# The prologue's first three tiles over tokens 0 to 255 and 256 to 575, and its loads, transposes and splits in a new order

## What is computed

```python
def rmsnorm(x, g):
    xf = x.astype(jnp.float32)
    xf = xf * lax.rsqrt(jnp.mean(xf * xf, axis=-1, keepdims=True) + EPS)
    return (xf * g.astype(jnp.float32)).astype(x.dtype)
...
    h = rmsnorm(x, norm_mix_g)
    p = h @ w_in
    u = jax.nn.gelu(p[..., :o1])
    v = rmsnorm(jax.nn.gelu(p[..., o1:o2]), sgu_norm_g)
```

## Time and profile before

| | |
|---|---|
| median of 3 runs | 2241.7 us (2239.98 to 2243.11) |
| the profiled execution | 2245.36 us, span 2243.7 us |
| TensorE busy | 2212.0 us of the span, 99% |
| VectorE, ScalarE, GpSimd busy | 79%, 50%, 24% |
| first matmul of tile 0 | 23.34 us |
| first matmul of tile 3 | 74.80 us |

### The profile page before, as it was taken

The page is one execution under the profiler, slowest core; times in us unless marked ns, Lnnn a source line. Parts: engine busy times, 40 slices in busy tenths (PEclk is TensorE's granted clock), DMA queues, the critical chain, the costliest instruction groups (busy, mean ns, idle before and its releaser), DMA issues.

```text
span 2243.7 us, 43356 instructions
## 1 busy us (share of the span) xinstructions
PE 2212.0 (99%) x16612; PEld 2198.8 (98%) x16612; DVE 1762.5 (79%) x2354; ACT 1112.1 (50%) x1758; POOL 547.0 (24%) x685
## 2 busy tenths in 40 slices
PE   8999999999999999999999999999999999999997
PEld 8999999999999999999999999999999999999997
DVE  5777678778335998888888888888887898888886
ACT  7554444444112554445444444444444665555565
POOL 3101112212222111111111111011112355555573
PEclk9999999999999999999999999999999999999998
DMA  8334445558333244435453535353536567765433
GB/s 258 105 110 132 117 128 156 176 171 261 114 96 107 81 148 136 153 124 154 132 158 114 164 123 159 115 167 120 157 121 243 193 207 242 235 215 201 167 105 105
DMA packets 377575, 346.05 MB, mean 154 GB/s; under 512 B 10474, under 2 KB 350629, under 8 KB 372720
## 3 DMA queue, kind: packets, MB, share of 16 engines
q1 hardware_dynamic: 346608, 203.98, 31.2%
q0 software_dynamic: 30848, 140.46, 17.4%
HBM read 273.40 MB, written 71.00 MB: 153 GB/s over the span
## 4 chain that ended last, share of the span: by engine, by line
PE 61%; DMA 1%; POOL 1%; DVE 1%; issue 0%; ACT 0%; POOLq 0%
PE ps L3043 14%; PE ps L3045 13%; PE ps L3044 13%; PE ps L3104 7%; PE ps L3106 7%; PE ps L3105 7%; DMA form<-act_scratch 1%; PE ps L3118 0%; DVE w_lo L2363 0%; POOL down L1029 0%; PE ps L3162 0%; PE ps L3164 0%; PE ps L3163 0%; POOL down_s L1028 0%; POOL X L1035 0%
## 5 line engine op out<-in xcount | busy, mean ns | idle before, releaser
L3104 PE MATMUL ps<-form,dw_hi 128*128 128x288 f32 x1204 | 358.5, 298 | 5.7 <-DVE dw_lo L2519 3.6
L3105 PE MATMUL ps<-form,dw_hi 128*128 128x288 f32 x1204 | 355.3, 295 | 0.0
L3106 PE MATMUL ps<-form,dw_lo 128*128 128x288 f32 x1204 | 354.7, 295 | 0.0
L2519 DVE TENSOR_TENSOR dw_lo<-down,dw_hi 128x512 fp32r<-128x512 f32 (+1 forms) x280 | 241.1, 869 | 73.9 <-ACT dw_hi L1131 73.1
L3043 PE MATMUL ps<-hq,w_hi 128*128 128x288 f32 x1008 | 298.0, 296 | 1.1 <-DVE w_lo L2363 1.1
L3044 PE MATMUL ps<-hq,w_hi 128*128 128x288 f32 x1008 | 296.7, 294 | 0.0
L3045 PE MATMUL ps<-hq,w_lo 128*128 128x288 f32 x1008 | 296.1, 294 | 0.0
L3104 PEld LDWEIGHTS ps<-form,dw_hi 128*128 128x128 f32 x1204 | 226.7, 188 | 7.3 <-DVE dw_lo L2519 4.3
L3105 PEld LDWEIGHTS ps<-form,dw_hi 128*128 128x128 f32 x1204 | 228.5, 190 | 0.0
L3106 PEld LDWEIGHTS ps<-form,dw_lo 128*128 128x128 f32 x1204 | 228.1, 189 | 0.0
L1131 ACT ACTIVATE dw_hi<-down 128x512 fp32r<-128x512 f32 (+1 forms) x280 | 166.1, 593 | 98.8 <-PE ps L3106 90.9
(11 more groups left out here) (417 smaller groups left out, 6466.9 us busy)
## 6 DMA issues: line engine op xcount, KB each, us to landing
raw<-in_w_gate_dram SPq DMA_DIRECT2D x88, 512.0 KB, 4.8
down<-in_w_down_dram SPq DMA_DIRECT2D x32, 1024.0 KB, 5.5
form<-act_scratch POOLq DMA_DIRECT2D x28, 1152.0 KB, 7.1
act_scratch<-stage POOLq DMA_DIRECT2D x45, 576.0 KB, 5.1
raw<-in_w_in_dram SPq DMA_DIRECT2D x42, 512.0 KB, 5.4
raw_c<-in_w_up_dram SPq DMA_DIRECT2D x42, 512.0 KB, 3.8
raw_d<-in_w_up_dram SPq DMA_DIRECT2D x42, 512.0 KB, 5.0
raw<-in_w_out_dram SPq DMA_DIRECT2D x30, 512.0 KB, 4.0
```

What stands on the lines that cost most here:

```text
L2519: v.tensor_tensor(dw_lo[:, m % 4, 0:n], down_form(m // NQ, m % NQ), dw_hi[:, m % 4, 0:n].bitcast(F32), ALU.subtract).then_inc(lo_ready, 1)
L3104: te.matmul(out, dw_hi[:, m % 4, j, :], act_f[:, j, 0, :], start=start and j == 0, stop=False, skip_group_check=True)
L3105: te.matmul(out, dw_hi[:, m % 4, j, :], act_f[:, j, 1, :], start=False, stop=False, skip_group_check=True)
L3106: last = te.matmul(out, dw_lo[:, m % 4, j, :], act_f[:, j, 0, :], start=False, stop=stop and j == n - 1, skip_group_check=True)
```

## The change

The three plain tiles are cut at token 256 and no longer at 288: PRE_COLS gives 256 columns for the first half and 320 for the second, and the first half needs only x blocks 0 and 1. X_BANK is another. SP loads pieces 0 and 1 after x block 1 and before block 2, then waits for eight transposed units and loads raw_z, and after that x block 3 and the samples. TensorE transposes block 2 between parts 1 and 2 of tile 0 and block 3 after tile 1. ScalarE and VectorE have their work in another order; the high and low parts of units 8 to 11 come much later, and the squares of the samples come after pieces 4 and 5. Units 4 to 7 are copied to buffers of their own, xh_early, over x_nat of block 0, so that their copies wait for no store; pieces 4 and 5, whose high parts lie in the same place, wait for those stores.

```diff
@@ -242,7 +242,17 @@
         def pre_lo_of(q):
             return w_lo2[:, q - 4] if q in (4, 5) else w_lo[:, PRE_SLOT[q]]
 
-        X_BANK = (4, 5, 6, 7, 0, 1, 2, 3, 4, 5, 6, 7, 1, 3, 6, 7, 5, 6, 7, 5)
+        X_BANK = (4, 5, 6, 7, 1, 2, 3, 4, 5, 6, 7, 1, 3, 6, 7, 1, 5, 6, 7, 5)
+        PRE_COLS = (slice(0, 2 * P), slice(2 * P, T))
+        xh_early = sb("xh_early", [P, 4, 4 * P], at=n_at)
+
+        def stage_of(u):
+
+            return xh_early[:, u - 4] if 4 <= u < 8 else xh_stage[:, u % 4]
+
+        def pre_out(tile, half):
+
+            return ps[:, 2 * PRE_PAIR[tile] + half, 0:PRE_COLS[half].stop - PRE_COLS[half].start]
 
         def x_bank_before(u):
 
@@ -570,16 +580,15 @@
                     load(q + half, half, col(w, n, half), first=first)
 
             sp.dma_start(vec_nat[0:KT, :], norm_mix_g[0].rearrange("(t c) -> t c", c=P)).then_inc(gain_landed, 16)
-            for tb in range(TB + 1):
-                if tb < TB:
-                    sp.dma_start(x_nat[tb][:, :], xp[tb * P:(tb + 1) * P, :]).then_inc(xnat_landed[tb], 16)
-                else:
-                    sp.dma_start(x_nat[tb][0:SAMP, :], xs).then_inc(xnat_landed[tb], 16)
-                if tb == 2:
+            for tb in range(TB):
+                sp.dma_start(x_nat[tb][:, :], xp[tb * P:(tb + 1) * P, :]).then_inc(xnat_landed[tb], 16)
+                if tb == 1:
                     tile2(w_in, HEADS, 0, first=True)
-            sp.wait_ge(x_t, 8)
-            for s in range(2):
-                sp.dma_start(raw_z[:, s], col(w_in, HEADS + 1, s)).then_inc(rawz_landed[s], 16)
+                elif tb == 2:
+                    sp.wait_ge(x_t, 8)
+                    for s in range(2):
+                        sp.dma_start(raw_z[:, s], col(w_in, HEADS + 1, s)).then_inc(rawz_landed[s], 16)
+            sp.dma_start(x_nat[TB][0:SAMP, :], xs).then_inc(xnat_landed[TB], 16)
             for n in range(2, PRE):
                 for s in range(2):
                     sp.wait_ge(lo_ready, s + 1 if n == 2 else 2 * n - 1 + s)
@@ -721,7 +730,7 @@
                                 ).then_inc(late_landed, 16)
                 pool.wait_ge(xT_copied, u + 1)
                 g.dma_start(scratch.rearrange("p (k t) -> p k t", k=KT)[:, 4 * kq:4 * kq + 4, tb * P:tb * P + n],
-                            xh_stage[:, u % 4, 0:4 * n].rearrange("p (k t) -> p k t", k=4)).then_inc(ring_out[u % 4], 16)
+                            stage_of(u)[:, 0:4 * n].rearrange("p (k t) -> p k t", k=4)).then_inc(ring_out[u % 4], 16)
             pool.wait_ge(frms_ready, TB + 1)
             g.dma_start(rms_scr[0:SEQ].rearrange("(t p) -> p t", p=P), rms_nat[:, 0:TB],
                         allow_slow_non_contiguous=True).then_inc(rms_out, 16)
@@ -1167,9 +1176,11 @@
                 for u in units:
                     n = P if u // 4 < TB else SAMP
                     act.wait_ge(xg_ready, u + 1)
-                    if u >= 4:
+                    if u >= 8:
                         act.wait_ge(ring_out[u % 4], 16 * (u // 4))
-                    a.activation(xh_stage[:, u % 4, 0:4 * n], ps[:, X_BANK[u], 0:4 * n], ACT.Copy).then_inc(xT_copied, 1)
+                    elif u >= 4:
+                        act.wait_ge(x_t, 4)
+                    a.activation(stage_of(u)[:, 0:4 * n], ps[:, X_BANK[u], 0:4 * n], ACT.Copy).then_inc(xT_copied, 1)
 
             def pre_hi(q, done):
 
@@ -1179,24 +1190,31 @@
                     act.wait_ge(rawz_landed[q - 2], 16)
                 else:
                     act.wait_ge(raw_landed[q % 2], 16 * (q // 2 + (1 if q < 2 else 0)))
+                if q in (4, 5):
+                    for n in range(2 * q - 8, 2 * q - 6):
+                        act.wait_ge(ring_out[n], 2 * 16)
                 a.activation(pre_hi_of(q), pre_raw(q), ACT.Copy).then_inc(hi_ready, 1)
 
-            for tb in range(3):
-                x_square(tb)
-            x_stage(range(0, 4))
-            x_hi(range(0, 8))
+            x_square(0)
+            x_square(1)
+            x_hi(range(0, 1))
             pre_hi(0, 0)
+            x_hi(range(1, 2))
+            x_stage(range(0, 1))
+            x_hi(range(2, 3))
             pre_hi(1, 0)
-            x_stage(range(4, 5))
-            x_hi(range(8, 12))
+            x_hi(range(3, 8))
+            x_square(2)
+            x_stage(range(1, 5))
+            pre_hi(2, 0)
+            pre_hi(3, 0)
             x_stage(range(5, 8))
-            pre_hi(2, 0)
             x_square(3)
-            pre_hi(3, 0)
             x_stage(range(8, 12))
-            x_square(4)
             pre_hi(4, 0)
             pre_hi(5, 0)
+            x_square(4)
+            x_hi(range(8, 12))
             x_stage(range(12, 16))
             x_hi(range(12, 16))
             x_hi(range(16, 17))
@@ -1209,8 +1227,9 @@
                 if t == 0:
                     for n in range(4):
                         act.wait_ge(ring_out[n], 16 * (TB + 1))
-                a.activation(ring[:, t, 0:HALF], pair(PRE_PAIR[t], 0), ACT.Gelu_apprx_tanh)
-                a.activation(ring[:, t, HALF:T], pair(PRE_PAIR[t], 1), ACT.Gelu_apprx_tanh).then_inc(tile_read, 1)
+                m = PRE_COLS[0].stop if t < 3 else HALF
+                a.activation(ring[:, t, 0:m], ps[:, 2 * PRE_PAIR[t], 0:m], ACT.Gelu_apprx_tanh)
+                a.activation(ring[:, t, m:T], ps[:, 2 * PRE_PAIR[t] + 1, 0:T - m], ACT.Gelu_apprx_tanh).then_inc(tile_read, 1)
 
             def v_square(i, *gelu_done):
 
@@ -1866,24 +1885,28 @@
             x_diag(0)
             x_gain(range(0, 1))
             x_diag(1)
-            x_gain(range(1, 6))
-            x_diag(2)
-            x_gain(range(6, 12))
-            for u in range(8):
-                x_lo(u)
+            x_gain(range(1, 8))
             pre_lo(0)
             pre_lo(1)
+            x_diag(2)
+            for u in range(4):
+                x_lo(u)
+                x_lo(u + 4)
+            pre_lo(2)
+            pre_lo(3)
+            x_gain(range(8, 12))
+            x_diag(3)
+            pre_lo(4)
+            pre_lo(5)
+            x_gain(range(12, 16))
+            x_diag(4)
             for u in range(8, 12):
                 x_lo(u)
-            x_diag(3)
-            pre_lo(2)
-            pre_lo(3)
-            x_gain(range(12, 16))
-            x_diag(4)
-            pre_lo(4)
-            pre_lo(5)
-            x_gain(range(16, 20))
-            for u in range(12, 20):
+            x_gain(range(16, 18))
+            for u in range(12, 16):
+                x_lo(u)
+            x_gain(range(18, 20))
+            for u in range(16, 20):
                 x_lo(u)
             v.tensor_copy(sel[:, :, :], ident[:, 0:NS].rearrange("p (a j) -> p a j", a=1).broadcast_to([P, NB, NS])
                           ).then_inc(sel_ready, 1)
@@ -2712,7 +2735,6 @@
             x_transposes(0)
             pe.wait_ge(vec_ready, 1)
             x_transposes(1)
-            x_transposes(2)
 
             def params_t():
                 pe.wait_ge(late_landed, 2 * 16)
@@ -2728,35 +2750,32 @@
                 te.matmul(ps[0:SAMP, 6, 0:SAMP], sel[:, :, :].rearrange("p b j -> p (b j)"), wsT[:, :, 0:NS],
                           start=True, stop=True).then_inc(corner_done, 1)
 
-            assert HALF <= 3 * P
-
             def pre_part(tile, half, part, kks=range(KT)):
 
-                cols = slice(half * HALF, (half + 1) * HALF)
                 for kk in kks:
                     s, k = kk // PK, kk % PK
                     q = 2 * tile + s
-                    unit = (4 * TB if half else 8) + kk // 4
                     if part == 0:
                         if k == 0:
                             pe.wait_ge(hi_ready, q + 1)
                         if kk % 4 == 0:
-                            pe.wait_ge(xhi_ready, unit + 1)
+                            pe.wait_ge(xhi_ready, (4 * TB if half else 4) + kk // 4 + 1)
                     elif part == 1:
                         if k == 0:
                             pe.wait_ge(lo_ready, q + 1)
                     elif kk % 4 == 0:
-                        pe.wait_ge(xlo_ready, unit + 1)
+                        pe.wait_ge(xlo_ready, 4 * TB + kk // 4 + 1 if half else 2 * (kk // 4 + 1))
                     w = pre_lo_of(q) if part == 1 else pre_hi_of(q)
                     x = h_lo if part == 2 else h_hi
-                    last = te.matmul(pair(PRE_PAIR[tile], half), w[:, k, :], x[:, kk, cols],
+                    last = te.matmul(pre_out(tile, half), w[:, k, :], x[:, kk, PRE_COLS[half]],
                                      start=part == 0 and kk == 0, stop=part == 2 and kk == KT - 1)
                     if part == 2 and half == 1 and k == PK - 1:
                         last.then_inc(piece_done, 1)
 
             for half in range(2):
                 for tile in range(3):
-                    pe.wait_ge(xT_copied, ((5, 7, 9), (13, 14, 20))[half][tile])
+                    if half or tile:
```

(5 more changed lines are left out.)

## The result

The kernel becomes slower: 2249.34 us median (20 runs, 2242.46 to 2252.38) against 2242.86 of the kernel before in the same comparison (20 runs), a ratio of 1.0027 with a 95% interval from 1.0019 to 1.0035, some 6 us. The forecast was no change, 2242.6. The profiled execution took 2248.56 us for a span of 2246.9.

The account below looks back on a forecast made before the run. TensorE, busy 99% of the span, was taken to bound the kernel. Terms -6.1 + 0.8 + 3.3 + 2.8 = +0.8 us on 2241.7, rounded up to 2242.6 us; likely 2241 to 2245, full range 2235.8 to 2247.5.

Parts of the forecast that it names:

- First tile's inputs: Prologue: earlier raw pieces start the first tile at 16.7, 0.8 us of idling replaces 4.1, clock stays up; -6.1 us.
- The backlog: DMA after 16.86 us: 5.5 MB of loads and stores land late, near 35 to 36, delaying ScalarE, VectorE and the fifth diagonal.
- the slower rival: ScalarE's copies wait behind late stores, with raw_z taking 9.6 us, delaying several units; +6.5 us, 2248.2 us; chance 0.18.
- Unit 13: Fourth block's transposes on TensorE: unit 13 waits for unit 9's copy, held by a store; 0.8 us lost.
- The pause: TensorE waits from 38.7 to 42.0 for the fifth diagonal; 3.3 us.
- Columns: Tile matmuls of 256 and 320 columns instead of 288: taken as 0, bounds +1.9 and -1.7 us.
- The clock: After the pause near 39, TensorE falls to 1.2 GHz for some 7 us; +2.8 us (2.0 to 3.4).
- Clock stays up: Rival: same new wait before the fifth diagonal, but no clock fall; -2.0 us, 2239.7 us; chance 0.22.
- no new wait: Rival: transfers land by 31, so TensorE keeps the prologue gain; -6.1 us, 2235.6 us; chance 0.18.
- a slower outcome: Whole-kernel measurement above 2246.2 us; chance 0.18.

Follow-up runs that it names:

- pause_then_dense: Changed kernel plus 24 unused products of 256 columns between the wait for the fifth diagonal and unit 16; ratio 1.0020 to the kernel before.
- fill: Changed kernel plus 26 unread identity transposes on TensorE in place of its pause before unit 16; 2240.25 us, ratio 0.9992 to the kernel before.
- order_both: Changed kernel with the fifth block's squares, scaling and diagonal ahead of pieces 4 and 5 on ScalarE and VectorE; 2243.39 us, ratio 0.9998 to the kernel before.
- x3_early_order: Changed kernel with fourth block and samples loaded before raw_z, and fifth block's work ahead of pieces 4 and 5; 2240.11 us, ratio 0.9989 to the kernel before.
- x3_early: Changed kernel with only the loads of the fourth block and samples moved ahead of raw_z; ratio 1.0018 to the kernel before.
- x3_early_order_2: Second run of the changed kernel with both the early fourth-block load and the fifth block's work moved ahead; 2240.81 us, ratio 0.9989 to the kernel before.
- before_pause_half: Kernel before, plus only a pause of TensorE before the second half of tile 0, where products follow; 2247.43 us in one profiled run.

## Why the prediction was wrong

Step by step. *First tile's inputs*: start 16.7 forecast, 16.90 measured; second tile through at 32.4, measured 32.52; no wait over 0.5 us and the clock up. Right. *The backlog*: the fourth store 35.0, measured 34.70; the fifth squares 37.4, measured 37.76; the fifth diagonal 41.4, measured 41.61. Right to 0.4 us. The DMA issues of the changed kernel show what held them (KB each, then us from issue to landing), for the stretches from 16.5 us (raw_z), 17.8 (the fourth x block), 19.8 (the reloads for pieces 4 and 5) and 23 (the stores of units 4 to 7):

```profile
raw_z<-in_w_in_dram SPq DMA_DIRECT2D x2, 512.0 KB, 5.4
```

```profile
x_nat<-in_x_prompt_dram SPq DMA_DIRECT2D x1, 1024.0 KB, 10.0
```

```profile
raw<-in_w_in_dram SPq DMA_DIRECT2D x2, 512.0 KB, 15.8
```

```profile
xT_scratch<-xh_early POOLq DMA_DIRECT2D x4, 256.0 KB, 7.1
```

The reloads took 15.8 us where the earlier trace rows has 4.9 for one with a short queue, and the stores 7.1 to 8.3 against 3.6, as beside x before. Raw_z, first in the queue, took only 5.4, not the 9.6 that the slower rival gave it. By the Trainium skill, "DMA: Bandwidth & Descriptors", section "Queues, rings and completion order", each DMA engine takes turns between the queues, packet by packet; that loads and stores are late together (15.8 and 7.1 us) agrees. One bound of this step doesn't come out of its rows: the best rate throughout, 350 GB/s, gives 35.9 us and not 34.5. *Unit 13*: 0.8 forecast; the 32 transposes from 32.52 end some 0.4 us late. *The pause*: 3.3 forecast, 0.26 + 2.83 measured. Right, with the engines and the order named.

*Columns*: taken at nothing. The products of 256 columns go at 120 ns (28.68 to 30.60 by sixteen), those of 320 at 147 (2.35 us for sixteen), together some 3.4 ns more than two of 131.7: +0.5 us over 144 pairs, between the bounds.

*The clock* is the step that failed. The prediction had the fall itself right, and wrote that one more stretch of 1.2 GHz "costs what the present one does, 2.8 us (2.0 to 3.4, by how much falls on the pause)", "for some 7 us". It lasted 17.1. The length of a stretch was taken over from one in which the products of tile 0 stood behind the pause. It measured 14.57 - 8.63 = 5.9 us in the four groups (the same groups at the upper clock from `pause_then_dense`) and 3.93 - 2.35 = 1.6 in the first sixteen products of 320 columns: **7.5 us, not 2.8**. The sum with the measured terms is -6.1 + 0.4 + 3.1 + 0.5 + 7.5 = +5.4, and the fourth tile is 5.5 late. That the length hangs on the work behind the pause is shown on both kernels, with and without the change: 13.7 to 17.1 us before the sample groups (five kernels, 7.5 us of cost in two of them that have 17.1), 3.4 before plain products (1.6 us of cost), 3.4 again with 24 products set between. The Trainium skill's "TensorE: Matmul & The Clock Gate", section "HAM oscillation", says that waits for DMA between groups of matmuls bring the throttle back each time. In the prologue the pause of 1.52 us and those of 2.3 and more agree, though they end on ScalarE and VectorE; pauses of 1.86 to 1.94 us at 9.5 us left the clock up.

*The rivals.* "Clock stays up" is what `fill` is, and "no new wait" is what `order_both` and `x3_early_order` are at the fourth tile (71.19 and 69.60, forecast 69), though neither comes near its 2235.6 us. The slower rival had the sign, and its 2248.2 us lies close to the measured 2249.34 by luck, for its mechanism was another: the last of the stores of units 4 to 7 had landed by 34.70, not after 38, and no sample unit waited behind unit 16. *Times*: a slower outcome had 0.18, and the range ended at 2247.5, because every case that paid for the clock paid the same 2.8 us, at most 3.4; a stretch longer than the present one was in none.

**What stays open.** From the fourth tile to 1691 us the distance to the kernel before changes by less than 1 us in three kernels (changed kernel +4.6 there, `order_both` -3.6, `fill` -3.3); at the end of the profiles it is +3.2, -1.9 and -7.5. Between 1691 and 1965 us the profiled executions part: the clock falls near 1725 to 1732 for 6.8 us (before, `order_both`), 3.4 (changed, `x3_early_order`) or not at all (`fill`, `x3_early`), and the waits for the loads and low parts of the down projection come to 4 to 7 us, each time divided differently. The two runs of `x3_early_order`, one kernel, have 3.4 and 6.8 us there. So executions of one kernel differ by such late falls. The two executions of `order_both` with a mean clock of 0.997 took 2233.93 and 2237.97 us, the nine with 0.995 took 2242.49 to 2246.07, and `fill` has 0.997 in nine of eleven. That goes with `order_both`, 3.6 us ahead at the mark, having the median of the kernel before; why most of its executions have the lower clock was not found. Nor was it found what, beside its length, makes a pause bring the clock down: 1.52 us did and 1.90 didn't, and of two waits of 2.0 us at the same place near 520 us one did (`x3_early_order_2`) and one didn't (`pause_then_dense`). That the 64-column transposes in the groups, and not their alternation with products, keep the clock down was not separated either.

## What to carry to other kernels

Price a pause of TensorE by what is issued right behind it: in front of dense products it cost 1.6 us beyond itself (2.8 in the kernel before, where a stretch lasted 6.8 us), in front of groups with 64-column float32 transposes 7.5. A pause that can't be removed can be filled with matmuls that nobody reads, or put before dense work; here that brought the fourth tile 8.2 and 3.7 us forward. When work is moved later to feed an earlier start, look for the next engine order that now ends in one small operation (here a 64 x 64 diagonal), and move this one in front of the long ones on every engine of its chain: on ScalarE alone it gave nothing, on VectorE alone 1.3 of the 2.8 us.

## What the runs showed of the hardware

- The granted clock stayed at 1.2 GHz for 17.1 us (43.0 to 60.0 in the changed kernel) while TensorE was busy in every stretch of the profile. It came back 3.4 us after the fall when plain products were issued (`before_pause_half`, `pause_then_dense`), and 6.8 or 3.4 us after it in front of tile 0 of the kernel before.
- Pauses of 1.5, 2.3, 2.8, 2.9, 3.0 and 3.3 us in the prologue were each followed by a fall, and so were waits of 2.0 to 2.4 us near 520. Waits of 0.25 and 0.66 us were not, nor pauses of 1.86 to 1.94 us at 9.5 us, nor one of 2.0 near 524. Between 1.5 and 2.1 us the length alone doesn't decide.
- Twenty-four superfluous products made the prologue 3.7 us shorter, and 26 superfluous transposes 8.2, 0.7 of each from an earlier diagonal.
